# Gate and up projections by seven block products instead of eight, the down projection as a second phase

## The reference

```
h = x + jnp.concatenate([att, y], axis=-1) @ w_out
f = rmsnorm(h, norm_ffn)
h = h + (jax.nn.silu(f @ w_gate) * (f @ w_up)) @ w_down
```

## Time and profile before

| | us |
|---|---|
| median of 3 runs | 3276.09 |
| lowest and highest run | 3270.78, 3276.7 |
| the profiled execution's own time | 3267.44 |
| its span | 3265.6 |
| first gate matmul, last down matmul (profile) | 1543.75, 3242.2 |

### The profile page before, as it was taken

The page is one execution under the profiler, slowest core; times in us unless marked ns, Lnnn a source line. Parts: engine busy times, 40 slices in busy tenths (PEclk is TensorE's granted clock), DMA queues, the critical chain, the costliest instruction groups (busy, mean ns, idle before and its releaser), DMA issues.

```text
span 3265.6 us, 53293 instructions
## 1 busy us (share of the span) xinstructions
PE 3057.1 (94%) x21743; PEld 2899.3 (89%) x21743; DVE 957.0 (29%) x1714; ACT 763.0 (23%) x1171; POOL 981.5 (30%) x406
## 2 busy tenths in 40 slices
PE   6999997899999996899999999999999999999997
PEld 6887996687777784899999999999999999999997
DVE  2322797434333432212221221221212121121223
ACT  4223222222222222223212121212121112112122
POOL 2322332111111110233333333333333333333331
PEclk8999998998889996899999999999999999999998
DMA  6322223444444443432222222222222222222221
GB/s 186 109 66 72 92 92 91 115 131 139 129 126 117 115 126 114 139 100 93 78 78 86 96 78 78 78 84 98 78 78 78 86 96 78 78 78 89 93 91 59
DMA packets 350273, 317.78 MB, mean 97 GB/s; under 512 B 39821, under 2 KB 319413, under 8 KB 348808
## 3 DMA queue, kind: packets, MB, share of 16 engines
q1 hardware_dynamic: 319368, 293.93, 29.0%
q10 hardware_dynamic: 30720, 21.05, 2.1%
HBM read 284.90 MB, written 31.43 MB: 97 GB/s over the span
## 4 chain that ended last, share of the span: by engine, by line
PE 57%; issue 34%; POOL 7%; ACTq 1%; DVE 1%; ACT 0%; POOLq 0%; DVEq 0%
PE G L705 40%; PE G L1117 17%; POOL WL L634 4%; POOL WL L663 3%; ACTq L1167 0%; ACTq L1168 0%; DVE us L2016 0%; DVE y_out L2035 0%; POOL WL L655 0%; ACT WRAW L1176 0%; PE B L720 0%; ACTq L39 0%; DVE gs L1987 0%; ACT XR L1181 0%; DVE hl L2022 0%
## 5 line engine op out<-in xcount | busy, mean ns | idle before, releaser
L705 PE MATMUL G<-AH,WH 128*128 128x288 f32 (+1 forms) x5024 | 1090.4, 299 | 42.0 <-DVE us L2016 12.2
L705 PE MATMUL G<-AL,WH 128*128 128x288 f32 (+1 forms) x5024 | 1077.9, 296 | 0.0
L705 PE MATMUL G<-AH,WL 128*128 128x288 f32 (+1 forms) x5024 | 1076.5, 296 | 0.0
L705 PEld LDWEIGHTS G<-AH,WH 128*128 128x128 f32 (+1 forms) x5024 | 814.2, 191 | 69.4 <-issue 51.3
L705 PEld LDWEIGHTS G<-AL,WH 128*128 128x128 f32 (+1 forms) x5024 | 814.9, 190 | 0.0
L705 PEld LDWEIGHTS G<-AH,WL 128*128 128x128 f32 (+1 forms) x5024 | 813.4, 190 | 0.0
L655 POOL TENSOR_TENSOR WL<-WRAW,WH 128x1024 fp32r<-128x1024 f32 x208 | 517.4, 2488 | 943.6 <-ACT WH L648 943.6
L648 ACT CAST WH<-WRAW 128x1024 fp32r<-128x1024 f32 x208 | 218.5, 1051 | 1006.6 <-PE G L705 900.1
L653 POOL TENSOR_TENSOR WL<-WRAW,WH 128x1024 fp32r<-128x1024 f32 x88 | 210.8, 2395 | 357.9 <-ACT WH L646 357.9
L1117 PE MATMUL G<-hh,WH 128*128 128x288 f32 x1408 | 303.0, 296 | 4.6 <-DVE hl L2022 4.6
L1117 PE MATMUL G<-hl,WH 128*128 128x288 f32 x1408 | 300.3, 294 | 0.0
(11 more groups left out here) (308 smaller groups left out, 2018.9 us busy)
## 6 DMA issues: line engine op xcount, KB each, us to landing
WRAW<-in_w_gate SPq DMA_DIRECT2D x22, 2048.0 KB
WRAW<-in_w_up SPq DMA_DIRECT2D x22, 2048.0 KB
WRAW<-in_w_down SPq DMA_DIRECT2D x22, 2048.0 KB
WRAW<-in_w_in SPq DMA_DIRECT2D x14, 2048.0 KB, 8.6
raw<-in_w_in SPq DMA_DIRECT2D x48, 512.0 KB, 4.0
kca<-in_cache_k SPq DMA_DIRECT2D x256, 64.0 KB, 2.0
vca<-in_cache_v SPq DMA_DIRECT2D x256, 64.0 KB, 2.0
WRAW<-in_w_out SPq DMA_DIRECT2D x16, 1024.0 KB
```

The source lines that it names most:

```text
L705: last = nc.tensor.matmul(G[gslot][0:width, h, 0:HALF], wt[:, half, k % 8, 0:width], act[:, (k + shift) % KT, h * HALF:(h + 1) * HALF], st ...
```

## The change

Gate and up are made first, for all 5632 hidden features, and down after them. A pair of output tiles (256 columns of w_gate or w_up) is one step q; even steps are gate, odd ones up, 44 in all. Its block of weights (2 x 2 quarters of 1024 x 128) and the activations (2 x 2 quarters of 1024 features x 288 tokens) are multiplied by seven products (`seventh`) instead of eight: products 0, 1, 4, 5 and 6 take a quarter of the weights (one of them replaced by a difference made in place), 2 and 3 take sums made by DVE; the seven activation operands xo (x00, x10, x11 and t1 to t4) are formed once. One product is 8 slices x 3 matmuls into one bank of F. Products 0, 2, 4 and 6 accumulate in bank 0, product 1 stands in bank 1, 3 and 5 in bank 2; ACT copies partial sums out (`keep`), DVE adds (`gather`) into gs2 or us2. WH, WL have a third place (W3). The norm is multiplied into the activations ahead of the products. In this phase DVE makes the weight remainders; GpSimd makes them for the output projection and for down only. The hidden product is stored to DRAM (hS, 576 KB for each pair of tiles) by SP and read back by groups of four tiles; the residual is stored tile by tile from ACT's queue (xrS) and read into XD as the down phase starts. `group_pe`, `group_act` and `group_dve` run the 11 down groups, with high and low hidden parts in two buffers H, made during the group before.

```
+        SET = 2 * 8 * HALF * 4
+        low, high, old = spot["AH"][0], spot["XR"][1], spot["XR"][0]
+        xo = {n: sb(f"xo_{n}", [P, 2, 8, HALF], F32R, at=at) for n, at in
+              (("x00", low), ("x10", low + SET), ("t1", low + 2 * SET), ("t2", low + 3 * SET), ("x11", high), ("t3", high + SET), ("t4", old))}
...
+        kept = sb("kept", [P, 3, HALF], at=high + 2 * SET)
+        gs2 = sb("gs2", [P, 2, NT], at=old + SET)
+        us2 = sb("us2", [P, 2, NT], at=spot["gs2"][1])
+        W3 = sb("W3", [P, 2, 8, P], F32R, at=spot["tokd"][0])
+        raw_l = sb("raw_l", [P, 2, 8, P], at=spot["WL"][0])
+        raw_3 = sb("raw_3", [P, 8, P], at=spot["W3"][0] + 4096)
+        diff = sb("diff", [P, 8, HALF], at=spot["xo_t1"][0] + SET // 2)
...
+        XD = sb("XD", [P, KT, NT], at=low + SET)
+        hraw = [sb("hraw0", [P, 4, NT], at=spot["us2"][1]), sb("hraw1", [P, 4, NT], at=old)]
...
+        PS = ctx.enter_context(nc.psum_tensor("PS", [P, 8, 512], F32))
+        G = [PS[:, 2 * i:2 * i + 2, :] for i in range(2)]
+        B = [PS[:, 4 + i, :] for i in range(4)]
+        F = [PS[:, 3 * i:3 * i + 3, :] for i in range(2)]
...
+            with sp.Fori(1, NPAIR // 2) as p:
+                for f, w in enumerate(("w_gate", "w_up")):
+                    sp.wait_ge(s["p_lo"], 14 * p + (7 * f - 7))
+                    to_slot(f, columns(w, p * 256))
+                store_hidden(p - 1)
+            sp.wait_ge(s["h_st"], 16 * (NPAIR // 2 - 1))
+            load_hidden(0, 0)
+            sp.wait_ge(s["p_lo"], NPROD - 7)
+            to_slot(0, down_rows(0, 0))
+            sp.wait_ge(s["p_done"], NPROD - 3)
+            for t in range(2):
+                sp.wait_ge(xr_st[t], 16 * (KT // 2))
+            for t in range(4):
+                sp.dma_start(XD[:, 4 * t:4 * t + 4, :], xrS[4 * t:4 * t + 4].rearrange("k p n -> p k n")).then_inc(xd_in[t], 16)
+            sp.wait_ge(s["p_lo"], NPROD)
+            to_slot(1, down_rows(0, 1))
+            sp.wait_ge(s["p_done"], NPROD)
+            load_hidden(1, 1)
...
+            store_hidden(NPAIR // 2 - 1)
+            sp.wait_ge(s["h_st"], 16 * (NPAIR // 2))
+            sp.wait_ge(s["w_lo"], CD + 4)
+            to_slot(0, down_rows(1, 0))
+            sp.wait_ge(s["w_lo"], CD + 8)
+            to_slot(1, down_rows(1, 1))
+            for g in range(2, NG):
+                sp.wait_ge(s["hl_done"], 4 * g - 4)
+                load_hidden(g, g % 2)
+                for d in range(2):
+                    sp.wait_ge(s["w_lo"], CD + 8 * g + 4 * d - 4)
+                    to_slot(d, down_rows(g, d))
...
+        def operand(up, j, r):
+            if j in (2, 3):
+                return w_raw(r)
+            return quarter(up, *((0, 0), (0, 1), None, None, (0, 0), (0, 1), (1, 1))[j])
...
+        OPERANDS = ("x00", "x10", "t2", "t1", "t3", "x11", "t4")
+        BANK = (0, 1, 0, 2, 0, 2, 0)
...
+            with pool.Fori(0, NG) as g:
+                for f in range(2):
                     for h in range(4):
-                        lower_p(pool, 24 * g + (C3 + 24 + 4 * f + h), h, f, f in (1, 2))
...
+            def seventh(c, q, j, r, up):
+                out = F[up][:, BANK[j], 0:HALF]
+                wh, wl, act = w_high(r), w_low(r), xo[OPERANDS[j]]
+                pe.wait_ge(s["p_lo"], c + 1)
+                if j == 0 and not (isinstance(q, int) and q < 2):
+                    pe.wait_ge(s["e_add"], 4 * q - 4)
+                if j in (2, 4, 5):
+                    pe.wait_ge(s["e_cp"], 3 * q + (1 if j == 2 else j - 2))
+                if j == 6:
+                    pe.wait_ge(s["e_add"], 4 * q + 2)
+                for k in range(8):
+                    for wt, m in ((wh, 0), (wh, 1), (wl, 0)):
+                        last = mm(out, wt[:, k, :], act[:, m, k, :], start=(j in (0, 1, 3) and k == 0 and wt is wh and m == 0), stop=(k == 7 and wt is wl), skip_group_check=True)
+                last.then_inc(s["p_done"], 1)
+            for c in range(14):
+                if c < 7:
+                    pe.wait_ge(s["x_lo"], X_READY[c])
+                seventh(c, c // 7, c % 7, c % 3, c // 7)
+            with pe.Fori(0, NPROD // 42) as it:
+                for n in range(42):
+                    seventh(42 * it + (14 + n), 6 * it + (14 + n) // 7, n % 7, (14 + n) % 3, n // 7 % 2)
+            def group_pe(g, b, after=None):
+                pe.wait_ge(s["hl_done"], 4 * g + 4)
+                for h in range(8):
+                    if isinstance(g, int) and g == 0 and h == 0:
+                        pe.wait_ge(s["e_add"], 4 * NPAIR)
+                    down_half(8 * g + (CD + h), h % 2, 16 * g + (TF + 2 * h), 2 * h, H[b])
+                    if after:
+                        after(h)
...
+            def weigh_x(n):
+                act.wait_ge(xr_st[n % 2], 16 * (n // 2 + 1))
+                actv(XR[:, n, :], XR[:, n, :], ACT.Copy, scale=gains[:, n:n + 1]).then_inc(s["x_g"], 1)
+            def cast(c, q, j, r, up):
+                if isinstance(c, int) and c < 2:
+                    act.wait_ge(s["w_used"], C3 + 31 + c)
+                elif not (isinstance(c, int) and c == 2):
+                    act.wait_ge(s["p_done"], c - 2)
+                if j == 0:
+                    act.wait_ge(w_ld[up], 16 * (q - up) + 160)
+                if j >= 2 and j < 6:
+                    act.wait_ge(s["p_raw"], 4 * q + (2, 4, 1, 3)[j - 2])
+                copy(w_high(r), operand(up, j, r)).then_inc(s["p_hi"], 1)
+            def keep(q, j, up):
+                n = {0: 0, 2: 1, 3: 2}[j]
+                act.wait_ge(s["p_done"], 7 * q + (j + 1))
+                if not (isinstance(q, int) and q == 0):
+                    act.wait_ge(s["e_add"], 4 * q - (3, 1, 2)[n])
+                copy(kept[:, n, :], F[up][:, BANK[j], 0:HALF]).then_inc(s["e_cp"], 1)
+            def gates(p):
+                act.wait_ge(s["e_add"], 8 * p + 4)
+                for t in range(2):
+                    actv(gs2[:, t, :], gs2[:, t, :], ACT.Silu).then_inc(s["p_silu"], 1)
+            def window(c, q1, j1, up1, q2, j2, r2, up2):
+                if j1 in (0, 2, 3):
+                    keep(q1, j1, up1)
+                cast(c + 2, q2, j2, r2, up2)
...
+            x_high("x00", x_part(0, 0), 1)
+            x_high("x10", x_part(1, 0), 2)
+            x_high("x11", x_part(1, 1), 4)
+            x_high("t1", diff[:, :, :], 5)
+            x_high("t3", x_part(0, 1), 6)
+            x_high("t2", x_part(0, 0), 7)
+            keep(0, 0, 0)
+            cast(3, 0, 3, 0, 0)
+            cast(4, 0, 4, 1, 0)
+            x_high("t4", x_part(1, 0), 8)
+            keep(0, 2, 0)
+            cast(5, 0, 5, 2, 0)
+            keep(0, 3, 0)
+            cast(6, 0, 6, 0, 0)
...
+            with act.Fori(0, NPROD // 42) as it:
+                for n in range(42):
+                    d = LOOP0 + n
+                    window(42 * it + d, 6 * it + (d - 1) // 7, (d - 1) % 7, (d - 1) // 7 % 2, 6 * it + (d + 2) // 7, (d + 2) % 7, (d + 2) % 3, (d + 2) // 7 % 2)
+                    if d % 14 == 8:
+                        gates(3 * it + d // 14)
...
+            def group_act(g, b, more=True, after=None):
+                for h in range(8):
+                    upper_d(g, h)
+                    if more and 2 <= h < 6:
+                        high_hidden(g + 1, 1 - b, h - 2)
+                    if after:
+                        after(h)
+            for j in range(4):
+                high_hidden(0, 0, j)
+            group_act(0, 0)
+            with act.Fori(0, (NG - 2) // 2) as it:
+                group_act(2 * it + 1, 1)
+                group_act(2 * it + 2, 0)
...
+            def low_w(c, j, r, up):
+                dve.wait_ge(s["p_hi"], c + 1)
+                tt(w_low(r), operand(up, j, r), w_high(r).bitcast(F32), ALU.subtract).then_inc(s["p_lo"], 1)
+            def difference(q, up):
+                a11 = quarter(up, 0, 0)
+                tt(a11, a11, quarter(up, 1, 0), ALU.subtract).then_inc(s["p_raw"], 1)
+            def second(q, r, up):
+                dve.wait_ge(s["p_raw"], 4 * q + 1)
+                tt(w_raw(r), quarter(up, 1, 1), quarter(up, 0, 0), ALU.subtract).then_inc(s["p_raw"], 1)
+            def fourth(q, r, up):
+                a12 = quarter(up, 0, 1)
+                dve.wait_ge(s["p_raw"], 4 * q + 2)
+                tt(a12, a12, w_raw(r), ALU.subtract).then_inc(s["p_raw"], 1)
+            def sum_w(q, r, up):
+                tt(w_raw(r), quarter(up, 1, 0), quarter(up, 1, 1), ALU.add).then_inc(s["p_raw"], 1)
+            def prepare(c, q, j, r, up, between=None):
+                if j in (2, 3):
+                    dve.wait_ge(s["p_done"], c - 2)
+                if j == 2:
+                    second(q, r, up)
+                    fourth(q, r, up)
+                if j == 3:
+                    sum_w(q, r, up)
+                if between:
+                    between()
+                low_w(c, j, r, up)
+                if j == 0:
```

(118 more changed lines are left out.)

232 lines of the change are left out of this document (107 added, 125 removed).

## The result

The changed kernel takes 3191.61 us (median of 4 runs, 3189.03 to 3192.87) against 3275.07 us for the kernel before in the same session (4 runs, 3270.78 to 3276.7): a ratio of 0.9746, 95% interval 0.9729 to 0.9763. Forecast 3178, range 3150 to 3222: inside, 13.6 us above the point. The profiled execution took 3192.23 us, its span 3190.4.

What follows compares the result with a forecast made beforehand. TensorE's matmul rate was taken as the bound. Products -132, start +38 and hand-over -4 sum to -98 us, giving 3178 us against the median of the kernel before; range 3150 to 3222.

Steps and rivals of the forecast that it cites:

- The products: Gate/up matmuls on TensorE: 1056 fewer, a product of 24 matmuls taking 3.17 us; gain 132 us.
- Who prepares the weights: DVE takes over GpSimd's weight remainders in the product phase: 16.0 us against 22.2 us of matmuls, hidden, costed at nothing.
- the full step: Third product of an up pair, fullest for DVE: about 6.1 us of preparation within 6.3, fits by 0.2 us.
- The start: Serial preparation of activations before the products: 47 us lost, 9 of them there before the change too, net +38.
- The turns: TensorE's loop turns: six in the first loop and three in the second, nine as before, costed at nothing.
- The hand-over and down: From products to down groups: 0.6 us and 2.1 us of stall against a removed gap and low clock, net -3.6 us.
- (b): Rival: DVE's fullest step in the product loop doesn't fit, or short waits at each product; 33 us more, 3211; 17%.
- (a): Rival: DVE sets the pace of the product loop, its passes costing 2.13 us; 168 us more, 3346; 4%.
- (c): Rival: TensorE takes the 288 columns at 120 ns in the products; 90 us less, 3088; 3%.
- (d): Rival: the activations' start or the hand-over's transfers cost double; 38 + 9 us more, 3225; 10%.

## Why the prediction came out as it did

The time from the end of the output projection to the end is the fair base: that end is at 1538.3 us before and 1541.8 after, in code that nobody changed (1539.0 to 1545.6 in the experiments), 3.5 us that belong to no step. Profile to profile the forecast was 22.8 us low (3192.2 against 3169.4); in the medians 13.6, since the profiled execution of before lies 8.7 us under the median it was set against, that of after 0.6 over its own.

- **The products:** right. 3.189 us on the mean against 3.17; over the 301 products from the eighth on, +5.7 us. That one bank takes all 24 matmuls costs nothing that can be seen: the spacing is 132.3 to 133.3 ns where 132.2 was taken. The differences between products are of place in SBUF, which no row of before showed.
- **Who prepares the weights:** right in the sum and in the margin (0.35 us where 0.2 were foreseen), wrong in the place of the full step. DVE's passes take 1.22, 0.755 and 0.453 us as read from the earlier trace rows. The hidden product goes out in one store of 576 KB for a pair of tiles, not in pieces of 288 KB; nothing hung on that.
- **The start:** eighth product at 67.0 us against 69, the first at 18.1 against 19, the third at 37.9 against 39, the fifth at 55.0 against 57. -2 us. The passes of 2304 elements take 2.56 us, ACT's 2.12, estimated 2.53 and 2.2. The chain put the low clock at the fifth product alone; the first and the third ran at it too (5.6 and 5.9 us), which cost nothing, as DVE's passes were behind them.
- **The turns:** the step that failed: "PE turns six times in the first loop and three times in the second, nine as before: nothing." The six cost 27.4 us where 9.6 were implied, +17.8 us. A turn was taken as a constant. It depends on how many instructions the body has (the three of the down loop cost nothing), on what the DMA engines carry while the instructions are fetched (3.6 or 5.4 us of branch) and on whether the pause is followed by a stretch at the low clock. The branch row of the kernel before (L1128, above) was in the trace and could have been read: 3.6 us, with the weight load at its end.
- **The hand-over and down:** forecast 0.6 + 2.1 us of stall, measured 0.85 and none, as the hidden tile came some two us sooner. A down group takes 51.2 us instead of 50.8 (133.5 ns a matmul in the chain against 132.2), which gives back what the three turns no longer cost. From the last product to the end -1.7 us in all.

Sum: 3.5 + 5.7 + 17.8 - 2 - 1.7 = 23.3, of 22.8 to be explained. The remaining 0.5 is within the rounding of the terms. Of the rivals, (b)'s number lay closest (3211), its mechanism is not in this kernel; (a), (c) and (d) did not come. That the result stands inside the range is luck in part: its upper end was widened for (b) and (d), and no term or width was meant for the turns, which took 17.8 us.

**Open:** why four of six turns are followed by the low clock and two aren't, at nearly the same gap (3.31 us with it, 3.14 and 3.34 without), why the later norm and the exchange of places make it more, and why gate and up groups of the kernel before take two lengths once its loop is written out.

## What to carry over

A hardware loop with a long body (here 2016 matmuls and weight loads or more) has a price at each turn, and that price depends on the transfers that run at that moment: look up the branch instruction of each engine in the trace, and either write the loop out, shorten its body below the length that is free, or put the turn where the queues are idle. When an elementwise pass is moved to another engine, take its duration from a row in which both engines work as they will afterwards. And a phase that begins with full-width passes over all activations pays for them in full: move out of its front what commutes with the products.

## What the runs showed of the hardware that was not expected

- A taken branch of TensorE takes 0.2 us with a body of 1536 matmuls and weight loads, 3.4 to 4.2 us at 2016 and 2304 when no load is under way or it ends soon after, 5.2 to 5.8 us when transfers go on for 3 us or more, up to 6.7 in the run with GpSimd, where the load begins later: a 16 KB packet of instructions starts only as the load runs out.
- After a gap of 3.1 to 3.8 us the granted clock is sometimes at its low level for 3.4 us, in some of the experiments 6.8 us; after the 1.5 us of the moved turns (five) and the 1.2 to 2.0 us of the kernel before (nine) it never was.
- The same 24 matmuls take 3.176 or 3.198 us by the place of the moving operand in SBUF.
- DVE passes with both inputs in SBUF that run beside GpSimd passes of 1024 elements take 1.8 to 2.3 times as long on the mean; with GpSimd at work in the loop nothing was left of the gain of this change.
- The end of a stretch that is the same in all these kernels moved between 1538.3 and 1545.6 us from one execution to another: differences of a few us are read from stage to stage, not from the span.
